# Two orders in a one-core encoder step: when VectorE forms the gated activation of an expert item, and when TensorE transposes a normed tile of the out-projection

## What is computed

```python
        x = x + g1 * out                       # out = mixed @ w_out
        h = _rmsnorm(x, wts['norm_ffn'][l]) * (1.0 + sc2) + sh2
        x = x + g2 * _moe(h, ...)
# in _moe, t = h as rows:
    s = jax.nn.sigmoid((t @ w_router).astype(jnp.float32))
    ...
    a = jax.nn.silu(jnp.einsum('nd,edf->nef', t, w_gate)) * jnp.einsum('nd,edf->nef', t, w_up)
    a = a * gates[:, :, None].astype(a.dtype)
    return jnp.einsum('nef,efd->nd', a, w_down).reshape(B, T, D)
```

## Time and profile before

| | |
|---|---|
| median of 3 runs | 1601.84 us (1598.27 to 1605.42) |
| the profiled execution | 1610.96 us, span 1609.2 us |
| mean granted TensorE clock | 0.926 of full speed |
| TensorE busy | 1400.7 us (87%) |
| VectorE busy | 1040.8 us (65%) |
| ScalarE busy | 866.2 us (54%) |
| GpSimd busy | 457.6 us (28%) |
| chain that ended last | TensorE 68%, VectorE 12%, issue 7%, DMA 5%, ScalarE 5% |
| moved by DMA | 357.59 MB, mean 222 GB/s |

### The profile page before, as it was taken

One profiled execution on the slowest core, in us unless ns is written; L12 is line 12 of the kernel. 1 busy time (PEld: TensorE's weight loads), 2 busy tenths in 40 slices (PEclk: granted clock), 3 DMA queues, 4 the chain that ended last, 5 costly groups with the idle time before them and its releaser, 6 DMA issues.

```text
span 1609.2 us, 27667 instructions
## 1 busy us (share of the span) xinstructions
PE 1400.7 (87%) x10165; PEld 1139.7 (71%) x10165; DVE 1040.8 (65%) x1445; ACT 866.2 (54%) x1545; POOL 457.6 (28%) x362
## 2 busy tenths in 40 slices
PE   5899999988749999999928999999794699999990
PEld 3688887757537777888828888887573577788870
DVE  1756642236458989889966444443555499898885
ACT  3344455462218777888733444443512377788872
POOL 1111121110025656666510000000000366566650
PEclk9799999989859999999968999999796699999995
DMA  9465633242328989999962643343505399999984
GB/s 313 118 214 182 207 114 113 76 170 80 148 86 314 355 332 347 371 374 385 377 200 61 176 148 114 113 124 114 184 18 212 120 334 353 340 359 365 372 322 185
DMA packets 167822, 357.59 MB, mean 222 GB/s; under 512 B 20770, under 2 KB 82978, under 8 KB 159026
## 3 DMA queue, kind: packets, MB, share of 16 engines
q1 hardware_dynamic: 155380, 331.94, 58.3%
q0 software_dynamic: 12352, 24.40, 4.3%
HBM read 340.56 MB, written 33.54 MB: 232 GB/s over the span
## 4 chain that ended last, share of the span: by engine, by line
PE 68%; DVE 12%; issue 7%; DMA 5%; ACT 5%; SPq 1%; DVEq 1%; ACTq 0%; POOL 0%; POOLq 0%
PE bank L609 16%; PE bank L611 15%; PE bank L610 15%; DVE ring_r L2108 4%; PE bank L320 3%; DMA ring<-in_w_down 2%; ACT work_r L2101 2%; PE bank L695 2%; PE bank L1550 2%; PE bank L1588 1%; PE bank L762 1%; PE bank L2400 1%; PE bank L1565 1%; DMA ring<-in_w_ada 1%; PE bank L1015 1%
## 5 line engine op out<-in xcount | busy, mean ns | idle before, releaser
L610 PE MATMUL bank<-ring_r,arena_r 128*128 128x512 f32 x816 | 322.3, 395 | 0.0
L2108 DVE TENSOR_TENSOR ring_r<-ring,work_r 128x1024 fp32r<-128x1024 f32 x102 | 182.4, 1814 | 20.7 <-ACT work_r L2101 20.7
L609 PE MATMUL bank<-ring_r,hT_r 128*128 128x384 f32 x512 | 185.5, 362 | 0.0
L2108 DVE TENSOR_TENSOR ring_r<-ring,arena_r 128x1024 fp32r<-128x1024 f32 x96 | 156.3, 1661 | 34.6 <-ACT arena_r L2101 34.5
L610 PEld LDWEIGHTS bank<-ring_r,arena_r 128*128 128x128 f32 x816 | 155.8, 191 | 30.5
L611 PE MATMUL bank<-ring_r,work_r 128*128 128x384 f32 x512 | 172.7, 337 | 0.0
L610 PE MATMUL bank<-ring_r,hT_r 128*128 128x384 f32 x512 | 172.3, 337 | 0.0
L2108 DVE TENSOR_TENSOR ring_r<-ring,hT_r 128x1024 fp32r<-128x1024 f32 x108 | 151.5, 1430 | 21.6 <-ACT hT_r L2101 20.7
L2101 ACT ACTIVATE hT_r<-ring 128x1024 fp32r<-128x1024 f32 x144 | 146.9, 1055 | 19.5 <-DMA ring<-in_w_gate 16.1
L2101 ACT ACTIVATE arena_r<-ring 128x1024 fp32r<-128x1024 f32 x128 | 127.6, 1052 | 35.6 <-DMA ring<-in_w_down 35.5
L2101 ACT ACTIVATE work_r<-ring 128x1024 fp32r<-128x1024 f32 x136 | 137.6, 1060 | 3.0 <-DMA ring<-in_w_up 2.7
(11 more groups left out here) (359 smaller groups left out, 2910.1 us busy)
## 6 DMA issues: line engine op xcount, KB each, us to landing
ring<-in_w_gate SPq DMA_DIRECT2D x136, 512.0 KB, 6.4
ring<-in_w_up SPq DMA_DIRECT2D x136, 512.0 KB, 6.2
ring<-in_w_down SPq DMA_DIRECT2D x68, 1024.0 KB, 8.0
bc<-in_w_ada SPq DMA_DIRECT2D x40, 1024.0 KB, 7.4
bc<-in_w_in_even SPq DMA_DIRECT2D x64, 192.0 KB, 5.6
bc<-in_w_in_odd SPq DMA_DIRECT2D x64, 192.0 KB, 3.6
arena<-moe_out SPq DMA_DIRECT2D x8, 1024.0 KB
ring<-in_w_ada SPq DMA_DIRECT2D x3, 2048.0 KB, 13.6
```

The source lines that it names most:

```text
L609: nc.tensor.matmul(acc, rows_hi, w_hi, start=first, stop=False)
L610: nc.tensor.matmul(acc, rows_hi, w_lo, start=False, stop=False)
L2108: dve.tensor_tensor(r32(piece(m_low[v], q)), piece(m_low[v], q), f32(piece(m_high[v], q)), ALU.subtract).then_inc(MO[f"lo_{c}"], 1)
```

## The change

In `out_pe`, both halves of the sample tile are done first. Then each tile j from 2 on has its first half, turn(j - 2), its second half, and logits(j - 2). For j = 4 the logits come later: after its second half follow turn(3), logits(2), logits(3), turn(4), logits(4). So turn(0) stands one full product later than before, and turns 1 and 2 are half a tile later too, each behind the first half of the next tile. In `moe_dve`, `product(n)` moves ahead of gate piece 0 and the row remainders of item n + 1, inside the loop's turn. The code after the loop, for the last item, is as it was. No instruction is added or removed.

```diff
             out_product(pe, l, 0, 0, OUT_KS[l][6:])
             out_product(pe, l, 1, 0, (5, 6, 7))
             out_product(pe, l, 0, 1, OUT_KS[l])
-            for j in range(1, TILES):
-                if j >= 2:
-                    out_product(pe, l, j, 0, OUT_KS[l])
+            out_product(pe, l, 1, 1, OUT_KS[l])
+            for j in range(2, TILES):
+                out_product(pe, l, j, 0, OUT_KS[l])
+                turn(j - 2)
+                out_product(pe, l, j, 1, OUT_KS[l])
+                if j < TILES - 1:
                     router_logits(pe, name, j - 2)
-                out_product(pe, l, j, 1, OUT_KS[l])
-                turn(j - 1)
+            turn(TILES - 2)
+            router_logits(pe, name, TILES - 3)
             router_logits(pe, name, TILES - 2)
             turn(TILES - 1)
             router_logits(pe, name, TILES - 1)
@@ moe_dve, turn(n, before)
                 if before:
                     split("d", n, 0, 2, 3)
+                product(n)
                 split("g", n + 1, 0)
                 rows_low(n + 1)
-                product(n)
                 split("g", n + 1, 2, 3)
                 split("u", n + 1, 0)
```

## The result

The changed kernel took 1618.15 us as a median of 7 runs (1612.28 to 1623.68), against 1601.84 us for the kernel before in the same series (7 runs, 1589.69 to 1605.42). The ratio is 1.0096, 95% interval 1.0069 to 1.0123: slower by about 1%. The forecast was 1585.2 us and the range ended at 1595. The profiled execution took 1623.68 us with a span of 1621.8 us, 12.6 us more than the span before. Some executions of a kernel are slower at a lower granted clock, whatever the kernel, and every median and ratio here leaves those out.

A forecast was written before the change was run, and what follows sets the result against it. TensorE, the busiest engine, was taken as the bound, its waits for VectorE as the loss. Terms -11.2 - 7.9 - 3.2 + 3.0 + 2.7 = -16.6 us took the 1601.84 us median to 1585.2 us; range 1577 to 1595.

The forecast's parts named there:

- Out-projection: In both layers, turn(0) one full product later ends TensorE's wait and clock loss there: 6.8 and 4.35 us, sum 11.2 us.
- evacuations late on VectorE: Out-projection: evacuation of turn(j-1) precedes tile j's scaling; for j = 2 VectorE waits some 4 us, with 9 us margin.
- the new logits: Out-projection tail: logits(2), 0.65 us, lies in TensorE's 3.56 us wait for ScalarE; without that cover, 0.65 us a layer.
- The long waits: Experts' first halves: the earlier product lets TensorE start gate 1.3 us earlier in six items, a gain of 7.9 us.
- The first items: First expert item of each layer: the product must wait for up, delaying gate; a loss of 1.5 us, twice, 3.0 us.
- The clock: Experts: shorter waits spare the clock's fall after one of three long waits in each layer, 1.6 us each, gain 3.2 us.
- items without a long wait: Experts: 0.4 us of VectorE's lead over GpSimd's split is left; five second-half items lose 5.3 us, half taken, 2.7 us.
- rival (c): Experts: GpSimd wins the port wherever VectorE now has it first; 24 items at 1.3 us, +15 us, 1617 us; chance 0.04.
- The bound by the DMA: Experts' first halves can't beat the DMA-full second halves, 127.3 us for seven items: at most 7.9 and 8.0 us a layer.
- Rival (b): Experts reach the second halves' pace at once, first items included: -27.1 us with the out-projection, 1575 us; chance 0.09.

The follow-up runs named there:

- e4: The changed kernel, with GpSimd's gate split inside the loop waiting until VectorE has made gate piece 0; 1586.14 us, ratio 0.9867.
- e7: e4 with VectorE making gate piece 0 before the product in the turn ahead of the loop, as in the kernel before; 1575.59 us, ratio 0.9809.
- e3: The changed kernel with VectorE's order gate piece 0, product, row remainders, and GpSimd as it was; 1586.57 us, ratio 0.9891.

## Why the prediction was wrong

**Out-projection: right.** Forecast 6.8 and 4.35 us, traces 7.4 and 5.0 us. No wait ahead of the first transposition, 1.03 us for it, products of 5.83 us, evacuations late on VectorE (it waited 3.6 and 4.95 us for them) with no price, the new logits in the cover of the wait ahead of the last ones (now 3.0 us). The tail was as before.

**The long waits: the mechanism right, the gain given back.** They went, as forecast. But the reckoning let every second item be a long one and the others stay free. Measured, most items take 19.15 us with 1.14 to 1.2 us of wait for the row remainders; the others take 17.75 us where piece 0 was free, and then one or two of 20.5 us follow. The first seven items of the loop in layer 0 took 132.8 us instead of 135.2, the eight after them 156.4 us instead of 145.5 us, which is 19.5 us an item instead of the 18.2 of the earlier trace rows. So the first halves gained a little, and the second halves lost 1.2 to 1.4 us an item.

**The first items: right, a little small.** Forecast a loss of 1.5 us each. The trace after has TensorE waiting 3.3 and 3.7 us there besides 0.9 us for the product, against 2.7 us before. Relative to the up product's end, the gate product starts 4.9 us later (478.60 to 483.49) against 3.15 us (485.67 to 488.82) in layer 0, which is 1.7 us, and 2.0 us in layer 1.

**The clock: wrong.** Forecast -3.2 us, for the two falls after long waits. Those two are gone, but items behind a free one wait 2.5 us at L609, and after each of these four waits the clock was down again (busy by stretch):

```profile
658.21:663.00 4.79, 4.79 (x14) 3.82 (x15) 4.79 (x3) 2.89 (x4) 3.23 (x2) 0.65 0.96 393
755.33:760.00 4.67, 4.67 (x14) 3.73 (x15) 4.67 (x3) 2.90 (x4) 3.22 (x2) 0.65 1.00 411
```

In layer 1 it was 0.66 from 1403.42 us and 0.69 from 1462.21 us. By the forecast's own 1.6 us for one, that is an estimated loss of 3.2 us instead of a gain of as much.

**The step that failed** is the one on items without a long wait: "VectorE's gate split starts 1.03 us before GpSimd's; the product takes 0.6 us of that (0.67 less the overlap), 0.4 us is left." The 0.4 us was indeed left (0.43 in the trace) and did not help. I read the start of GpSimd's record as the moment it asks. e4 and the free items show that it can have the port earlier, during the gather, when its piece has been rounded. The 1.03 us was no margin: the record of GpSimd's split starts where the gather ends. In the item of the earlier trace rows that was 541.51 + 1.15 = 542.66 us, 0.02 us before the split's 542.68:

```profile
541.51 1.15 POOL L2194 DMA_INDIRECT arena<-moe_in,now_tok  x1 [0.87 <-ACT hT_r L2101]
```

The experts lost 23.0 us against a forecast gain of 5.4 us, 28.4 us apart. Some 6 us of that are the clock's, behind waits that come from the same blocked pieces; put on this one term, it was 2.7 + 28.4 = 31 us instead of 2.7. The range had nothing for this step but those 2.7 us, so it ended 23 us short of the measured time.

So rival (c) came true: its place, and about its price of 1.3 us an item (measured 1.14 to 1.2 in most). Its count was too high: it let all 24 free pieces be blocked besides the six, and 25 of the 30 are, 19 more. That its 1617 us lies so close to the measured 1618.15 us is therefore partly luck. Its condition, "as soon as GpSimd asks within 0.6 us", fits as well, but it got a chance of 0.04 because I looked for that asking in the wrong column.

The Trainium skill (SBUF — State Buffer, Who interferes with whom) says "Issue order, not op shape, decides who blocks". The runs agree if issue is taken as issue: the split at 538.38 us blocked a piece asked for at 537.95. A record's start is not it.

**The bound by the DMA was set too tight for the first halves**, without effect on the result. I held that the experts can't go faster there than the second halves, 127.3 us for seven items. The first seven items of e4's loop in layer 0 took 124.82 us. In e7 (busy by stretch, in its first half and over seven items of its second):

```profile
520.00:640.00 120.00, 120.00 (x569) 100.58 (x569) 109.89 (x88) 101.11 (x123) 79.69 (x47) 1.00 1.01 376
641.25:768.66 127.41, 125.95 (x592) 104.26 (x590) 114.28 (x92) 105.03 (x127) 80.25 (x48) 1.00 1.00 379
```

In the first stretch TensorE is busy for all 120.00 us, at 17.75 us an item: its own pace. The items there move less: in the kernel before, seven of the first half moved 46.77 MB and seven of the second 47.87 MB, as the gathers and scatters are smaller. In its second half e7 is back at 18.2 us an item, as the kernel before was (127.30 us), and e4 took 125.26 us for seven. So nothing here shows that the transfers are no ceiling in the second halves. Rival (b) took 18.2 us as the floor everywhere; that its 1575 us is close to e7's median says little, as e7 is another kernel and its series had a kernel before of 1612.3 us.

What stays open: at which moment of the gather GpSimd takes the port. The free piece of e3, asked 0.15 us after the gather's start, and the blocked one 0.75 us after it are the two ends that the runs give. Nothing between them was tried, and so neither was a VectorE instruction of 0.6 us in the product's place that does use the port. Nor was it tried whether the port is claimed by the queued split or by some late part of the gather when a split follows; both fit, and both mean that the record's start is too late.

## What to carry to other kernels

Where two engines share a port, a piece asked for 0.6 us later can cost 2.7 us: here 0.15 us into the other engine's gather it was free, 0.75 us into it it was not. An unbroken row of port-using instructions is no protection by itself. Read a contender's readiness from what it waits for (here ScalarE's rounding), not from its record's start, and if the order matters, fix it with a semaphore: one wait on GpSimd (with the old order kept for the first item) turned the order that lost 1% into one that gained 2%. And move a transposition behind work that is ready, not behind what it depends on: one product later was worth 12 us, idle time and lost clock at one place per layer.

## What the runs showed of the hardware that was not expected

- GpSimd's split blocks VectorE before its own record starts: piece 0 asked for at 537.95 us ran only after the split that is recorded from 538.38 to 540.79 us. It did so in the items in which its weights had been rounded 0.26 us or more before VectorE asked, and not where that was 0.17 us or less.
- A gather that is being issued does not by itself hold the port: piece 0 took 1.21 us in its middle (539.36 in a gather from 538.61 to 539.76 us).
- The record of a GpSimd split that is queued behind a gather, its piece rounded, starts where the gather ends (0.02 to 0.03 us after it in the items shown), whatever VectorE does at the time: in the changed kernel it starts 0.43 us after the ask both where VectorE has the port and where GpSimd has it. Waiting for the port lies inside the record (3.06 us against 2.41 us).
